# Sparse attention of a fused two-block kernel: per-head keys and values in place of latent ones, and another order of its softmax

## The reference, cut to what matters

```python
q = (c_q @ w_uq).reshape(B, T, A_HEADS, A_HEAD_DIM)
q_lat = jnp.einsum('bthd,hdc->bthc', q, w_uk) * (A_HEAD_DIM ** -0.5)
...
rel = jax.nn.relu(jnp.einsum('bqhd,bsd->bqhs', qb_idx, k_idx))
score = jnp.einsum('bqh,bqhs->bqs', wb, rel).astype(jnp.float32)
score = jnp.where(key_pos[None, None, :] <= q_pos[None, :, None], score, -jnp.inf)
_, sel = lax.top_k(score, n_sel)
...
bias = rel_bias[t5_bucket(dist)].transpose(0, 1, 3, 2)
logits = jnp.einsum('bqhc,bqkc->bqhk', qb_lat, kv_sel) + bias
logits = jnp.where((dist >= 0)[:, :, None, :], logits, -jnp.inf)
p = jax.nn.softmax(logits, axis=-1)
o_lat = jnp.einsum('bqhk,bqkc->bqhc', p, kv_sel)
...
o = jnp.einsum('bthc,hcv->bthv', o_lat, w_uv).reshape(B, T, A_HEADS * A_V_DIM)
return o @ w_o
```

## Time and profile before

| | us |
|---|---|
| median of 3 runs | 2865.66 |
| lowest, highest | 2864.12, 2866.37 |
| the profiled execution, its own time | 2866.46 |
| its span (first to last instruction) | 2864.7 |

### The profile page before, as it was taken

The page is one execution under the profiler, slowest core; times in us unless marked ns, Lnnn a source line. Parts: engine busy times, 40 slices in busy tenths (PEclk is TensorE's granted clock), DMA queues, the critical chain, the costliest instruction groups (busy, mean ns, idle before and its releaser), DMA issues.

```text
span 2864.7 us, 36987 instructions
## 1 busy us (share of the span) xinstructions
PE 2730.5 (95%) x14045; PEld 2338.0 (82%) x14045; DVE 1891.3 (66%) x3534; ACT 1193.5 (42%) x1927; POOL 537.9 (19%) x393
## 2 busy tenths in 40 slices
PE   8999999989998999999998999999999989999997
PEld 6787878878877999999997888888888547788886
DVE  3334765755555778786985889888887496444434
ACT  5445243233213454547994333333333445322322
POOL 0122220220000678772000112111110011000000
PEclk9999999999999999999999999999999999999999
DMA  4112101003562677775668889988984200232220
GB/s 163 52 52 89 59 30 45 30 30 116 216 226 90 226 288 281 279 248 200 258 243 297 338 328 352 339 329 333 347 320 145 83 30 21 90 103 103 88 103 30
DMA packets 141359, 501.19 MB, mean 175 GB/s; under 512 B 13400, under 2 KB 67072, under 8 KB 111616
## 3 DMA queue, kind: packets, MB, share of 16 engines
q1 hardware_dynamic: 122752, 364.60, 35.7%
q0 software_dynamic: 18432, 134.23, 11.9%
HBM read 450.53 MB, written 48.25 MB: 174 GB/s over the span
## 4 chain that ended last, share of the span: by engine, by line
PE 78%; DVE 11%; ACT 4%; DMA 3%; issue 2%; POOL 1%; SPq 0%; DVEq 0%; POOLq 0%; ACTq 0%
PE bank L247 21%; PE bank L249 21%; PE bank L248 21%; DVE xn L1534 2%; PE bank L2157 2%; DMA w_raw<-in_w_in_dram 2%; PE bank L1119 1%; PE bank L1109 1%; PE bank L1125 1%; PE bank L742 1%; DVE M L2947 1%; DVE whl L243 1%; DVE m L2943 1%; ACT whl L237 1%; PE bank L2745 1%
## 5 line engine op out<-in xcount | busy, mean ns | idle before, releaser
L247 PE MATMUL bank<-HH,uhl 128*128 128x384 f32 x1024 | 345.7, 338 | 1.9 <-POOL uhl L1660 1.9
L249 PE MATMUL bank<-HH,uhl 128*128 128x384 f32 x1024 | 342.8, 335 | 0.0
L248 PE MATMUL bank<-HL,uhl 128*128 128x384 f32 x1024 | 342.6, 335 | 0.0
L247 PE MATMUL bank<-vhl,awhl 128*128 128x512 f32 x768 | 301.1, 392 | 11.8 <-DVE awhl L2374 10.8
L249 PE MATMUL bank<-vhl,awhl 128*128 128x512 f32 x768 | 300.7, 392 | 0.0
L248 PE MATMUL bank<-vhl,awhl 128*128 128x512 f32 x768 | 300.7, 391 | 0.0
L1716 POOL DMA_INDIRECT gs<-in_uv_dram,idx x128 | 154.1, 1204 | 770.5 <-DVE x L1741 477.8
L2314 ACT ACTIVATE vhl<-vraw 128x1024 fp32r<-128x1024 f32 x128 | 135.7, 1061 | 321.8 <-PE bank L249 283.9
L1660 POOL TENSOR_TENSOR uhl<-ur,uhl 128x1024 fp32r<-128x1024 f32 x69 | 168.0, 2446 | 319.8 <-ACT uhl L1654 319.6
L243 DVE TENSOR_TENSOR whl<-w_raw,whl 128x2048 fp32r<-128x2048 f32 x49 | 114.6, 2339 | 160.3 <-ACT whl L237 160.3
L247 PE MATMUL bank<-HH,whl 128*128 128x512 f32 x528 | 213.7, 405 | 4.7 <-DVE whl L243 4.0
(11 more groups left out here) (421 smaller groups left out, 6241.3 us busy)
## 6 DMA issues: line engine op xcount, KB each, us to landing
ur<-in_peer_u_dram SPq DMA_DIRECT2D x128, 512.0 KB, 5.2
vraw<-in_peer_v_dram SPq DMA_DIRECT2D x128, 512.0 KB, 6.2
w_raw<-in_w_in_dram SPq DMA_DIRECT2D x36, 1024.0 KB, 5.0
xn<-in_ada_rows_dram SPq DMA_DIRECT2D x48, 512.0 KB, 4.7
g_scratch<-stg SPq DMA_DIRECT2D x12, 2048.0 KB, 7.9
gti<-g_scratch SPq DMA_DIRECT2D x16, 1536.0 KB, 11.8
wf_raw<-in_f_w_in_dram SPq DMA_DIRECT2D x22, 1024.0 KB, 4.8
act_scratch<-ag SPq DMA_DIRECT2D x96, 192.0 KB, 2.8
```

What stands on the lines that cost most here:

```text
L247: e.matmul(out, l[0], r[0], start=start, stop=False)
L248: e.matmul(out, l[0], r[1], start=False, stop=False)
L249: return e.matmul(out, l[1], r[0], start=False, stop=stop)
```

## The change

- Latent form gives way to per-head form: `pe_up2` makes queries and keys of a head (4 products of 512 columns, two for each), a score is one product instead of two, `pe_v` makes the values of all heads (8 blocks), and the output of a head is four products of 512, 384, 256 and 128 columns straight into the output bank. `ql`, `ol`, `ov` and `crow` go.
- Logits are kept negated. The bias of the farthest bucket is taken off the table (a constant within a softmax), so only the nearest 256 columns have a bias; POOL adds it to the scores while DVE still chooses (`pool_near`). After the mask one `tensor_tensor_reduce` adds it and takes the row's minimum.
- The reciprocals are not multiplied into the probabilities. POOL scales an identity tile with each (`pool_share`), and PE turns the exponentials by a product with that diagonal (`pe_pt`) instead of a transpose. DVE copies two of a head's four turned tiles, ACT two.
- The scores of all heads are made before the steps. The 48 steps issue masks and exponentials three heads ahead of the turned copies. The value blocks and the first turnings stand on PE between scores and outputs; ACT copies two value blocks ahead of its first exponential and six within the steps.
- The index loop has the head outside and the block inside; two of the four index query projections move in front of heads 2 and 4.
- `M`'s first block is cleared and made causal by POOL at the start.

In the diff, removed lines of functions that were replaced are left out (they stand above).

```diff
...
+    dg = new.sb("dg", [P, 16, P])
+    vkv = new.sb("vkv", [P, NT, D])
...
+    qi = vf[:, 0:4 * S].rearrange("p (m t) -> p m t", m=4)
+    hank = vf[:, 4 * S:8 * S].rearrange("p (a c d) -> p a c d", a=8, c=2)
+    lm_last = new.sb("lm_last", [P, 6, 1280])
     with ExitStack() as ph:
...
+        qk2 = new.sb("qk2", [P, 2, 2, S], side="right")
...
+        lm_first = new.sb("lm_first", [P, 3, 1280], side="right")
...
+    slot = lambda i: lm_first[:, i, :] if i < 3 else lm_last[:, i - 3, :]
...
         e.dma_start(rb[:, :], a["rel_e"]).then_inc(*m_land.up("rel"))
...
     R9x = Ring(banks)
     moff = [0, 128, 384, 768]
     mw = [128, 256, 384, 512]
...
+    NI, STEPS = 32, 48
+    poff = [0, 512, 896, 1152]
+    pw = [512, 384, 256, 128]
     def item(g):
         return g // 4, (0, 3, 1, 2)[g % 4]
...
+    def tile(g):
...
+        return slot(h + 1)[:, moff[tb]:moff[tb] + mw[tb]]
+    def of_block(h, tb):
+        return 4 * h + (0, 2, 3, 1)[tb]
+    def turned(h, s_):
+        return slot(h)[:, poff[s_]:poff[s_] + pw[s_]]
+    def pe_up2(e, h, what, W, x):
...
+        i.then_inc(*T.up(what, h))
+    def act_up2(e, h, what, i, scale):
...
+        if h >= 2:
+            e.wait_ge(*T.of("sc", 4 * (h - 2) + 3))
+        e.wait_ge(*T.of(what, h))
+        e.activation(qk2[:, h % 2, i, :], R9.bank(what, h)[:, :], ACT.Copy, scale=scale).then_inc(*R9.out(A, what, h))
+    def pe_v(e, s_, half):
...
+            i = e.matmul(b[:, :], ckT[:, k, blk(s_)], W3.tile(W_UV)[:, k * D + half * 512:k * D + half * 512 + 512],
...
+        i.then_inc(*T.up("v", s_, half))
+    def act_v2(e, s_, half):
...
+        e.wait_ge(*T.of("v", s_, half))
+        e.activation(vkv[:, s_, half * 512:half * 512 + 512], R9.bank("v", s_, half)[:, :],
+                     ACT.Copy).then_inc(*R9.out(A, "v", s_, half))
...
+        e.wait_ge(*A.of("k", h))
+        e.matmul(b[:, 0:N], qk2[:, h % 2, 0, blk(tb)], qk2[:, h % 2, 1, 0:N], start=True, stop=True).then_inc(*T.up("sc", g))
...
+        e.activation(tile(g), R9.bank("sc", g)[:, 0:mw[tb]], ACT.Copy).then_inc(*R9.out(A, "sc", g))
+    def pool_near(e, g):
...
+        n = min(mw[tb], 256)
+        near = tile(g)[:, mw[tb] - n:mw[tb]]
+        e.wait_ge(*A.of("sc", g))
...
+                        ALU.add).then_inc(*G.up("near", g))
+    def dve_logits(e, g):
...
+        e.wait_ge(*G.of("near", g))
+        e.tensor_tensor_reduce(out=tile(g), in0=tile(g), in1=M[:, moff[tb]:moff[tb] + mw[tb]], scale=1.0, scalar=3.0e38,
+                               op0=ALU.add, op1=ALU.min, accum_out=st[:, 0, g:g + 1]).then_inc(*V.up("low", g))
...
+        e.wait_ge(*V.of("low", g))
+        e.activation(tile(g), tile(g), ACT.Exp, scale=-1.0, bias=st[:, 0, g:g + 1],
+                     accum_out=st[:, 1, g:g + 1]).then_inc(*A.up("ex", g))
+    def dve_inv(e, i):
...
+        e.wait_ge(*A.of("ex", 2 * i + 1))
+        e.reciprocal(st[:, 2, 2 * i:2 * i + 2], st[:, 1, 2 * i:2 * i + 2]).then_inc(*V.up("inv", i))
+    def pool_share(e, g):
...
+        if g >= 16:
+            e.wait_ge(*T.of("pt", g // 4 - 4, NT - 1))
+        e.wait_ge(*V.of("inv", g // 2))
+        e.tensor_scalar(dg[:, g % 16, :], ident, st[:, 2, g:g + 1], None, ALU.mult).then_inc(*G.up("share", g))
+    def pe_pt(e, h, s_):
...
+        if s_ == 0:
+            e.wait_ge(*G.of("share", 4 * h + 3))
+        for tb in range(s_, NT):
+            g = of_block(h, tb)
+            i = e.matmul(b[:, blk(tb - s_)], tile(g)[:, blk(s_)], dg[:, g % 16, :], start=True, stop=True)
+        i.then_inc(*T.up("pt", h, s_))
+    def act_pt(e, h, s_):
...
+        e.wait_ge(*T.of("pt", h, s_))
+        e.activation(turned(h, s_), R9.bank("pt", h, s_)[:, 0:pw[s_]], ACT.Copy).then_inc(*R9.out(A, "pt", h, s_))
+    def dve_pt(e, h, s_):
...
+        e.wait_ge(*T.of("pt", h, s_))
+        e.tensor_copy(turned(h, s_), R9.bank("pt", h, s_)[:, 0:pw[s_]]).then_inc(*R9.out(V, "pt", h, s_))
+    def pe_o(e, h):
...
+        e.wait_ge(*A.of("v", NT - 1, h // 4))
+        e.wait_ge(*V.of("pt", h, 1))
+        e.wait_ge(*A.of("pt", h, 3))
+        for s_ in range(NT):
+            i = e.matmul(b[:, s_ * P:S], vkv[:, s_, blk(h)], turned(h, s_), start=s_ == 0, stop=s_ == NT - 1,
+                         skip_group_check=True)
+        i.then_inc(*T.up("o", h))
+    def act_o(e, h):
...
+        e.wait_ge(*T.of("o", h))
+        e.activation(HH[:, h, :], R9.bank("o", h)[:, :], ACT.Copy).then_inc(*A.up("o", h))
+    def dve_o(e, h):
...
+        e.wait_ge(*A.of("o", h))
+        e.tensor_tensor(HL[:, h, :], R9.bank("o", h)[:, :], r32(HH[:, h, :]), ALU.subtract).then_inc(*R9.out(V, "o", h))
...
+        def pe_qi(m):
...
                 i = e.matmul(b[:, :], W3.tile(W_QI)[:, k * 512 + m * P:k * 512 + (m + 1) * P], cqT[:, k, :],
...
             i.then_inc(*T.up("qi", m))
...
+        pe_qi(0)
+        pe_qi(1)
+        for h in range(8):
+            if h in (2, 4):
+                pe_qi(h // 2 + 1)
+            pp = slice(64 * (h % 2), 64 * (h % 2) + 64)
+            e.wait_ge(*A.of("qi", h // 2))
+            for tb in range(1, NT):
...
                 e.matmul(b[:, 0:N], qi[pp, h // 2, blk(tb)], kiT[pp, 0:N], start=True,
...
+        for h in range(2):
...
+            pe_up2(e, h, "k", W_UK, ckT)
...
         for g in range(4):
...
+        for h in range(2, 10):
+            for g in range(4 * h - 8, 4 * h - 4):
+                pe_sc(e, g)
             if h < 8:
...
+                pe_up2(e, h, "k", W_UK, ckT)
...
+        for half in range(2):
+            for s_ in range(NT):
+                pe_v(e, s_, half)
+        for h in range(9):
+            if h < 8:
+                for s_ in range(NT):
+                    pe_pt(e, h, s_)
+            if h:
+                pe_o(e, h - 1)
...
+        e.wait_ge(*V.of("o", 7))
...
+        def act_qi(m):
...
+        act_qi(0)
+        act_qi(1)
...
+        for h in range(8):
+            for tb in range(1, NT):
+                if h:
+                    e.wait_ge(*V.of("ix", tb, h - 1))
...
                 e.activation(rl[n % 3][:, 0:mw[tb]], R9.bank("ix", tb, h)[:, 0:mw[tb]],
...
+            if h in (1, 3):
+                act_qi((h + 3) // 2)
+        for h in range(2):
+            act_up2(e, h, "q", 0, -(P ** -0.5))
+            act_up2(e, h, "k", 1, 1.0)
         for g in range(4):
...
+        for h in range(2, 10):
+            for g in range(4 * h - 8, 4 * h - 4):
...
             if h < 8:
...
+                act_up2(e, h, "q", 0, -(P ** -0.5))
+                act_up2(e, h, "k", 1, 1.0)
         e.preload_act_table_set(LN_SET)
+        act_v2(e, 0, 0)
+        act_v2(e, 1, 0)
         for s in range(STEPS):
...
                 act_exp(e, s)
...
+            if s % 3 == 1 and s <= 16:
+                n = (s + 5) // 3
+                act_v2(e, n % 4, n // 4)
+            if s % 4 >= 2 and 12 <= s < 44:
+                act_pt(e, s // 4 - 3, s % 4)
+            if s % 4 == 3 and s >= 16:
+                act_o(e, s // 4 - 4)
+            if s == 12:
+                e.wait_ge(*G.of("near", NI - 1))
                 split_hi(e, W3, W_O)
...
+            if s == 28:
+                e.wait_ge(*T.of("o", 2))
                 split_hi(e, W3, W_O + 1)
...
+        for h in range(8):
+            for tb in range(1, NT):
+                mo = M[:, moff[tb]:moff[tb] + mw[tb]]
...
+        e.tensor_scalar(M[:, P:1280], M[:, P:1280], -1.0e38, -MASKED, ALU.is_gt, ALU.mult).then_inc(*V.up("M"))
+        e.wait_ge(*G.of("M0"))
         e.wait_ge(*V.of("M"))
...
         for s in range(STEPS):
...
+                dve_logits(e, s)
+            if s % 2 and 3 <= s < NI + 2:
+                dve_inv(e, (s - 3) // 2)
+            if s % 4 < 2 and 12 <= s < 44:
+                dve_pt(e, s // 4 - 3, s % 4)
+            if s % 4 == 0 and s >= 20:
+                dve_o(e, s // 4 - 5)
+            if s == 14:
                 split_lo(e, W3, W_O)
...
+            if s == 30:
                 split_lo(e, W3, W_O + 1)
...
+        dve_o(e, 7)
         split_lo(e, W3, W_O + 2)
         split_lo(e, W3, W_O + 3)
...
+            tm = vkv[:, tb % 2, :]
...
                             ALU.mult).then_inc(*V.up("gated", tb))
...
+        e.memset(M[:, 0:P], 0.0).then_inc(*G.up("zero"))
+        e.wait_ge(*G.of("zero"))
+        e.affine_select(out=M[:, 0:P], in_=M[:, 0:P], pattern=[[-1, P]], compare_op=ALU.is_ge, fill=-MASKED, base=0,
+                        channel_multiplier=1).then_inc(*G.up("M0"))
         for tb in range(1, NT):
             d = M[:, moff[tb] + mw[tb] - P:moff[tb] + mw[tb]]
             e.wait_ge(*V.of("ix", tb, 7))
             e.affine_select(out=d, in_=d, pattern=[[-1, P]], compare_op=ALU.is_ge, fill=MASKED, base=0,
                             channel_multiplier=1).then_inc(*G.up("masked", tb))
...
         for g in range(NI):
...
+            pool_near(e, g)
+        for g in range(NI):
+            pool_share(e, g)
...
```

(52 more changed lines are left out.)

223 lines of the change are left out of this document (32 added, 191 removed).

## The result

The changed kernel takes 2820.14 us, median of 6 runs (2816.95 to 2821.94), against 2865.14 (2861.55 to 2866.37) of the kernel before on the same chip: ratio 0.984, 95% interval 0.983 to 0.986. It is faster by 1.6%, clear of the noise: by 45.0 us where 42.2 was forecast. The profiled execution took 2821.64 us, its span 2819.9.

A forecast was written before the change was run, and what follows sets the result against it. DVE was taken as the bound up to the mask, PE behind it. First output at 2353.6, 30.7 us of outputs and turnings, waits and tail put the projection at 2389.2 instead of 2431.44: gain 42.2, forecast 2823.5 us, range 2812 to 2838.

The forecast's parts named there:

- 11.6 a head: PE's work per head behind the mask in the kernel before, called the bound there; 4.4 us after the change.
- The sum: Addition of times from PE's first turning at 2346.5 to the projection's start at 2389.2, instead of 2431.44.
- index part: PE's index products with two query projections before the mask: 16.7 plus some 2 us for mode changes, ending at 2284.6.
- only the last pass of a head can lie beside the next head: Index products on PE: one head's passes queue on one array half; 1.93 us alone, 1.50 with a neighbour.
- the 2 us put: Index stage on PE: guess for five changes between full and half array, between 0 and 4 us.
- The start of the second half: After the mask: PE's second value block, out at 2336.2, releases ACT's first exponential at 2337.0; PE, not DVE, opens it.
- First output: First output product on PE: starts at 2353.6, after DVE's copies, splitting and reciprocal, then an exponential and last copy.
- The clock: Rival: PE at half clock after an idle spell, over outputs and turnings; costs up to 30.7 us; chance 0.05 with like losses.
- the 2.5 us for hand-overs and for contention between POOL and DVE: Stretch of outputs and turnings: 1.5 us for hand-overs on PE, one more us for DVE behind POOL.
- The 0.9 before a late output: PE's wait for the last exponential of head 7, with splitting at step 28/30 in front of it.
- the slower case: Rival: DVE's 32 fused add-and-minimum steps at 1.94 us each cancel the gain, beyond that slower; 2874 at 2.2; chance 0.02.
- The rival with DVE as the bound: After the mask: POOL's diagonals hold each fused step up by 0.4, DVE 6.05 a head; gain 33.2, 2832.5 us; chance 0.20.

The follow-up runs named there:

- The same-half order: Changed kernel with index heads ordered 0, 2, 4, 6, 1, 3, 5, 7 (even heads first, then odd), so neighbours use the same array half; 2818.18 us.
- The filler run: Changed kernel with 14 extra unused fp32 128x128 products on PE in its idle spell before the first output; stage 55.37 against 58.24 us, time 2816.09 us.
- the run with late splittings: Changed kernel with the two weight splittings moved behind the exponentials, ACT steps 32 and 36, DVE 34 and 38; stage 52.46 against 58.24 us.
- folding undone: Changed kernel with DVE multiplying exponentials by reciprocals and PE turning them by plain transposes, without POOL's diagonals; stage 59.12 us, time 2820.28 us.

## Why the prediction was right, and where it was not

Right in place and mechanism: only the attention stage changes, PE is the bound behind the mask, and the gain is PE's shorter work there. The forecast's "11.6 a head" for the kernel before holds only while the scores of the other four heads are made. From the timeline of PE before, the second latent output of two such heads, 12.2 apart:

```profile
2367.17 2.40 PE L2745 MATMUL bank<-PT,crow 128*128 128x128 f32 x20
...
2379.36 2.40 PE L2745 MATMUL bank<-PT,crow 128*128 128x128 f32 x20
```

From the fifth head on they are 9.3 to 8.1 apart. The sum did not use the 11.6, so nothing hangs on it. By the forecast's own prices the products that PE turns and outputs with behind the mask fall from 75.7 us (scores 17.3, latent outputs 36, up-projections 13.6, transposes 8.8) to 35.2. 17.3 of these 40 are scores that are now made ahead of the mask. The per-head form takes away another 32.3 (49.6 to 17.3), and turning by products instead of transposes gives 9.1 back. That is an estimate by count: no run takes back the one and keeps the other.

The rest is terms of the sum. The forecast instant is 3.0 late where its index part alone was 4.9 too long; 1.4 of that was lost again before the first output, 0.5 behind it.

| term | forecast | measured |
|---|---|---|
| index products and two queries, PE | 18.7 | 13.8 |
| mask made | 2334.2 | 2331.96 |
| value blocks end | 2346.5 | 2341.73 |
| first output starts | 2353.6 | 2350.18 |
| first output to end of last, with waits | 34.1 | 34.7 |
| projection starts | 2389.2 | 2386.24 |

- Index products. The step "only the last pass of a head can lie beside the next head" failed: a pair of heads on different halves takes 2.67, 1.4 less than two on the same half, where 0.43 less was put, and the 48 passes take 9.98 for 13.3. The changes between half and full array are about 0.2 each: 0.20 a group of index products, and 1.92 for a query between them where 1.72 is its own length. Five make 1.0 of the 2 us put. DVE's first maximum therefore came at 2283.71, not near 2286.0, and the mask with it. The same-half order is what the model described, and measured 14.7. (The Trainium skill, TensorEngine Tiling (Array Packing), "Key Properties", says that different tiles run in parallel; the trace agrees, 0.19 against 0.34 a pass. A drain at a change of mode, which it also states, costs here no more than those 0.2 us each.)
- The start of the second half. PE doesn't open it: the second value block is copied while the mask is made (2331.63), and the first exponential starts 0.3 after the first fused step (2332.43, forecast 2337.0).
- First output. The sum had DVE as its last step. What came last was the bank of the last value block, which ACT releases at step 16, behind an exponential that waits for a fused step behind DVE's splitting. Of the 4.8 us by which the value blocks end earlier this lost 1.4 again. I had counted ACT's copies as hidden and not asked who waits for their banks.
- The clock. The rival had the right sign and the wrong size: 2.6 us behind the spell of 3.37, not up to 30.7, and from 2357 on the granted clock stayed at 1.00, with no wait over 0.98 until the last output was made. The filler run shows it by itself. The sum had the clock at nothing.
- Of the 2.5 us for hand-overs and for contention between POOL and DVE only 0.4 can be found. The period is the bare sum, 2.23 + 2.16. So the last stretch came out nearly right by luck, by two errors that cancel: 2.1 too many, 2.6 for the clock missing. The 0.9 before a late output was right in size (0.98), but stands before the fifth, behind the second splitting, as the run with late splittings shows.
- The fused step, the operation without a row: 0.68 at 512 columns, its accumulator read of 0.08 hidden; some 1.8 a head at its pitch, forecast 2.2. With copies 1.07, reciprocals 0.16 and subtraction 0.6, DVE needs 3.6 a head, not 4.15. The condition of the slower case, 1.94 us a step on average, was over four times the measured 0.45.
- The rival with DVE as the bound failed on its price: POOL's diagonals stretch a fused step of 384 columns from 0.553 (folding undone, POOL still) to 0.603, 0.05 where 0.4 was put; one step of 256 columns went from 0.40 to 0.55. It is POOL that waits. A diagonal takes 0.60, but one that starts with a fused step of 384 or 512 columns takes 0.97 to 1.12, as here in the changed kernel (timeline of all engines):

```profile
2358.76 0.59 DVE L2695 CUSTOM_DVE_ANT_0 lm_last<-lm_last,M 128x384 f32<-128x384 f32 x1
2358.76 0.98 POOL L2714 TENSOR_SCALAR dg<-cst,st 128x128 f32<-128x128 f32 x1
```

  (The Trainium skill, SBUF — State Buffer, "Who interferes with whom", states the exclusion; the trace agrees, but nearly all of the cost lands on POOL, which isn't the bound.)
- The diagonals cost 0.60 alone and 0.84 on average, above both bounds (0.17 and 0.45), which came from another operation. It did no harm, since POOL had room for it, but the run with twice as many shows how little was left.

What isn't settled: how the gain divides between the per-head form and the scores made ahead of the mask; why a diagonal costs more than a two-input addition of the same shape; and why one spell of 3.38 us (diagonals doubled) was followed by no slow product while one of 2.46 was.

## What to carry to other kernels

Ask of each copy out of PSUM not only who reads its result but whose bank it frees: the wait that ended last here hung on a copy whose data nobody needed yet. Before trading work between engines, get the waits out of the in-order queues; the splittings put in front of short steps cost 5.8 us, more than the trade of diagonals for transposes in three heads could give. A spell without work on PE can cost more than its length: behind nearly every spell of 2.46 us or more in these runs the next products lost another 1.5 to 3.1 us at 1.2 GHz, behind the spells up to 1.68 us nothing.

## What the runs showed of the hardware

- Index products over 64 rows: 0.34 us a pass of mixed 256, 384 and 512 columns on one half, 0.19 to 0.22 when heads alternate between halves, whether the alternation is by product or by head.
- In six kernels PE's next output after a spell of 2.46 to 4.47 us without a product took 3.8 to 4.4 us instead of 2.16, at a granted clock of 0.50 where it was read; then the rate came back by itself. The loss doesn't follow the spell's length: 3.37 us cost 2.6 in the changed kernel and 1.6 with even heads first. With the diagonals doubled a turning behind 4.94 us took 3.75 instead of 2.23, and one behind 3.38 us was not slow (clock 1.00). After spells of up to 1.68 us the next output took 2.15 to 2.24.
- A diagonal that POOL makes beside DVE's 2.29 us splitting (both inputs in SBUF) stretches to 2.7, with the diagonals doubled to 2.9 and 3.0; the splitting takes 2.29 with POOL still as well (folding undone). POOL, and then DVE, timelines of the changed kernel; the first diagonal of the two takes 0.6:

```profile
2366.96 3.30 POOL L2714 TENSOR_SCALAR dg<-cst,st 128x128 f32<-128x128 f32 x2 [1.67 <-DVE st L2707]
```

```profile
2367.58 2.29 DVE L243 TENSOR_TENSOR wfhl<-wf_raw,wfhl 128x2048 fp32r<-128x2048 f32 x1
```
